# Latent stage of a hybrid layer on Trainium2: key latents first, query latents scaled after their product, sample queries on column groups

## The chip, the cores and the metric

The kernel runs on one core of one Trainium2 chip (trn2). The metric is device time in microseconds of one execution, lower is better. The core has five engines that matter here, each with its own instruction queue: TensorE (PE; its weight loads are listed as PEld), VectorE (DVE), ScalarE (ACT), GpSimd (POOL) and SyncE (SP), which issues the transfers between memory and the on-chip SBUF. TensorE writes into PSUM banks of 512 float32 columns.

## The reference

The program is a step of a small trunk of two layers over 288 tokens, 256 of a prompt and 32 of samples (8 sequences of 4). Each layer mixes three branches (a state-space branch "ssd", a recurrent branch "rwkv" and latent attention "mla") and ends in a feed-forward part. All branches read the same normalised rows through slices of one matrix `w_in`. What the change touches is the way from these rows to queries, keys and values:

```python
def rmsnorm(x, g, eps=NORM_EPS):
    y = xf * lax.rsqrt(jnp.mean(xf * xf, axis=-1, keepdims=True) + eps)
    return y * g

def mla_queries(cq, pos, q_a_g, w_q_b, q_norm_g):
    q = jnp.einsum('btr,rhe->bthe', rmsnorm(cq, q_a_g), w_q_b)
    q = jnp.concatenate([q[..., :MLA_NOPE], rope(q[..., MLA_NOPE:], pos)], axis=-1)
    return rmsnorm(q, q_norm_g)
...
    h = rmsnorm(x, p['norm_mix_g'])
    u = h @ p['w_in']
    q = mla_queries(u_mla[..., :MLA_Q_RANK], pos, p['mla_q_a_g'], p['mla_w_q_b'], p['mla_q_norm_g'])
    ckv = rmsnorm(u_mla[..., MLA_Q_RANK:MLA_Q_RANK + MLA_KV_RANK], p['mla_kv_a_g'])
    kpe = rope(u_mla[..., MLA_Q_RANK + MLA_KV_RANK:], pos)
```

The model width is 1024, the query rank 512, the key rank 256, the rotary part 64; there are 8 heads of 128 + 64. The ssd branch takes from `w_in` also 16 columns `dt`, one for each of its heads. The rwkv branch's output y (1024 features a token, 16 heads of 64) is normalised head by head, scaled, a bonus is added and the sum multiplied by a gate.

## The kernel before

`layer_program` runs the stages of a layer one after the other, in a loop over two layers; between two stages all engines meet. The stages that matter are, in order: `rwkv_tiles` (the recurrent scan), `mla_project` (called the latent stage here), `mla_qkv`, the attention stages, and later `ssd_project` and `ssd_tiles`.

Activations are kept transposed, features on the 128 partitions and 288 tokens along the row, and so are the latents. A float32 product of `w_in` columns with the rows is made of three passes over rounded halves (`product`, L301: weight head by row head, weight head by row rest, weight rest by row head). Each megabyte of weights (8 tiles of 128 rows, 256 columns) is fetched by SP, rounded by ScalarE into heads (a CAST), and split by VectorE into rests (a subtraction). A **unit** is 128 output features: 8 tiles x 3 passes = 24 matmuls of 288 columns.

The latent stage makes seven units in this order: four of query latents, two of key latents, and one for the rotary key (its 64 columns are loaded twice to fill 128). ScalarE copies each result from PSUM and squares it (L473, L474); TensorE sums the squares over features with a matrix of ones (L428, 6 instructions, each shown as 2 records since a plain float32 matmul takes two passes); ScalarE makes the inverse roots with Ln and Exp (L479, L481), each of which needs its own table loaded (ACT_TABLE_LOAD); VectorE applies gain and root to all six (L550). The key latents and the rotary key are turned token-major (L439, L434), the rotary key is rotated on VectorE (L541 to L546) and turned back (L444). SP writes both to memory, two stores for each (L383 to L387), and it also gathers ten cache pages in this stage (`gather_pages`). Between the units the recurrent branch's y is finished: mean and centring on VectorE (L520 to L522), squares on ScalarE (L462), inverse roots (L465, L467), scaling (L531), 32 transposes of 64x64 for each of two token tiles (`turn_y`, L399), then gain (L508), bonus (L513) and gate (L514). The first quarter of the first weights is fetched in `rwkv_tiles` (L2925) into `mla_w_first`.

`mla_qkv` makes keys, values and queries of three token tiles (two of 128 prompt tokens, one of the 32 samples; the samples need only queries). For a query tile, 12 matmuls (24 records) of 512 columns read `cqT`, the scaled query latents, as stationary operand. In the order of TensorE: keys and values of tiles 0 and 1, queries of tiles 0, 1 and 2, and then 64 transposes (`turns`, L621) whose results ScalarE copies out (L674, L676). Between a query pass and these turns, ScalarE keeps the queries (L654), VectorE rotates them (L695 to L700), ScalarE squares (L658), VectorE sums (L712), ScalarE makes inverse roots (L662, L664), and VectorE scales queries and keys (L714, L715). Each engine takes its instructions strictly in the order of the code.

`ssd_project` makes 10 double units and, as the eleventh load of 1 MB, one unit whose first 16 output features are dt (`dtT`, L1549).

## Time and profile before

| | us |
|---|---|
| median of 3 runs | 2954.49 |
| lowest, highest | 2952.33, 2960.16 |
| span of the profiled execution | 2949.8 |
| time of the kernel outside the span (median less span) | 4.7 |
| latent stage, layer 1 and layer 2 | 50.6, 51.73 |
| mla_qkv, layer 2 | 61.7 |

| engine | busy us | share of the span |
|---|---|---|
| TensorE | 2693.6 | 91% |
| VectorE | 1872.8 | 63% |
| ScalarE | 1352.8 | 46% |
| GpSimd | 841.2 | 29% |

A line of the timeline gives the start in the span, the time that a group of like instructions took, engine and source line, operation, what it writes and reads, the shapes, the count, and in brackets the idle time of the engine before it with the work or transfer that ended it. "x12" of a float32 matmul means six instructions. A releaser "PEq L232" is the meeting of the engines between two stages.

### The profile page before, as it was taken

Reading aid. Unit: us, or ns where it says so; the run is one execution under the profiler, and the core shown is the slowest. Engines: PE = TensorE matmul, PEld = TensorE weight load, DVE = VectorE, ACT = ScalarE, POOL = GpSimd, SP = SyncE. Lnnn points to the kernel's source line nnn. Section 1 sums busy time; section 2 is a strip of 40 time slices with the busy share of each in tenths; the row PEclk is TensorE's granted clock in tenths of the full one; section 3 lists DMA queues with packets and bytes.
Section 4 is the critical chain, followed back from the end, with each engine's and each line's share of the span. In section 5 each row is a group of like instructions: output and inputs, shape, how many; then the busy total and the mean of one; then the engine's idle time right before and its main releaser. Section 6 shows DMA issues by size and latency. Waiting matters only on the chain. (4 is left out here: it accounts for less than half of the span.)

```text
span 2949.8 us, 62087 instructions
## 1 busy us (share of the span) xinstructions
PE 2693.6 (91%) x24092; PEld 2462.7 (83%) x24092; DVE 1872.8 (63%) x3117; ACT 1352.8 (46%) x2294; POOL 841.2 (29%) x696
## 2 busy tenths in 40 slices
PE   7987889999999899899989878799999998998998
PEld 6876459999989689899978764599999895998998
DVE  4854457777766655489448454577777676554893
ACT  4733354545444244354357333555554442533542
POOL 0030009999910400000000300199999004000000
PEclk9999989999998999999989999899999998999999
DMA  5423459677545376365453243696866344764544
GB/s 134 110 59 105 138 100 148 117 129 122 83 79 161 97 202 168 104 166 139 126 115 101 65 132 112 115 141 115 139 106 104 74 141 124 199 172 108 161 133 120
DMA packets 838374, 365.86 MB, mean 124 GB/s; under 512 B 406189, under 2 KB 825558, under 8 KB 837512
## 3 DMA queue, kind: packets, MB, share of 16 engines
q1 hardware_dynamic: 835858, 360.77, 53.7%
q8 instruction: 184, 3.01, 0.4%
q10 hardware_dynamic: 2232, 1.26, 0.2%
q14 instruction: 100, 0.82, 0.1%
HBM read 342.63 MB, written 61.23 MB: 137 GB/s over the span
## 5 line engine op out<-in xcount | busy, mean ns | idle before, releaser
L1213 PE MATMUL key_banks<-w_kb_head,latent_T_head 128*128 128x352 f32 x1536 | 519.5, 338 | 9.7 <-DVE latent_T_rest L1341 9.7
L1213 PE MATMUL key_banks<-w_kb_head,latent_T_rest 128*128 128x352 f32 x1536 | 497.1, 324 | 0.0
L1213 PE MATMUL key_banks<-w_kb_rest,latent_T_head 128*128 128x352 f32 x1536 | 496.6, 323 | 0.0
L297 DVE TENSOR_TENSOR w_rests<-w_ring,w_heads 128x2048 fp32r<-128x2048 f32 (+1 forms) x150 | 321.6, 2147 | 146.9 <-ACT w_heads L291 146.7
L1355 DVE TENSOR_REDUCE w_kb<-key_sq 128x8 f32<-128x1024 f32 x256 | 311.2, 1216 | 12.4 <-ACT key_sq L1278 7.7
L1213 PEld LDWEIGHTS key_banks<-w_kb_head,latent_T_head 128*128 128x128 f32 x1536 | 290.5, 189 | 23.5 <-DVE latent_T_rest L1341 11.6
L1213 PEld LDWEIGHTS key_banks<-w_kb_rest,latent_T_head 128*128 128x128 f32 x1536 | 290.9, 189 | 0.0
L1213 PEld LDWEIGHTS key_banks<-w_kb_head,latent_T_rest 128*128 128x128 f32 x1536 | 289.8, 189 | 0.0
L291 ACT CAST w_heads<-w_ring 128x2048 fp32r<-128x2048 f32 (+1 forms) x150 | 268.4, 1792 | 42.8 <-ACT conv_last_rows L1934 19.7
L1033 POOL TENSOR_TENSOR rwkv_state_tmp<-rwkv_state,vec 128x1024 f32<-128x1024 f32 x64 | 153.3, 2395 | 455.6 <-POOLq L232 450.7
L1265 ACT CAST latent_T_head<-turn_bank 128x256 fp32r<-128x256 f32 x256 | 95.3, 372 | 400.6 <-PE key_banks L1217 392.2
L1278 ACT ACTIVATE key_sq<-key_banks 128x1056 f32<-128x1056 f32 x256 | 271.4, 1060 | 7.8 <-PE key_banks L1217 7.8
L2861 POOL TENSOR_TENSOR L_level<-L,const 128x1024 f32<-128x1024 f32 x12 | 28.1, 2366 | 793.5 <-DVE L L2867 793.5
L1341 DVE TENSOR_TENSOR latent_T_rest<-turn_bank,latent_T_head 128x256 fp32r<-128x256 f32 x256 | 108.2, 423 | 211.2 <-ACT latent_T_head L1265 211.0
L304 PE MATMUL ffn_banks<-h_heads_T,w_heads 128*128 128x288 f32 x704 | 212.8, 302 | 18.2 <-DVE h_rests_T L1950 13.8
L305 PE MATMUL ffn_banks<-h_rests_T,w_heads 128*128 128x288 f32 x704 | 209.6, 298 | 0.0
L306 PE MATMUL ffn_banks<-h_heads_T,w_rests 128*128 128x288 f32 x704 | 208.8, 297 | 0.0
L1036 POOL TENSOR_TENSOR rwkv_state_tmp<-rwkv_state_tmp 128x512 f32<-128x512 f32 (+4 forms) x320 | 197.9, 618 | 25.1
L304 PE MATMUL merge_banks<-out_heads,w_heads 128*128 128x288 f32 x512 | 150.9, 295 | 10.2 <-DVE out_rests L1751 5.2
L304 PEld LDWEIGHTS ffn_banks<-h_heads_T,w_heads 128*128 128x128 f32 x704 | 133.4, 189 | 22.8 <-DVE w_rests L297 18.0
L306 PE MATMUL merge_banks<-out_heads,w_rests 128*128 128x288 f32 x512 | 151.1, 295 | 0.0
L305 PE MATMUL merge_banks<-out_rests,w_heads 128*128 128x288 f32 x512 | 151.1, 295 | 0.0
(597 smaller groups left out, 7006.1 us busy)
## 6 DMA issues: line engine op xcount, KB each, us to landing
w_ring<-in_ffn_w_up_dram SPq DMA_DIRECT2D x88, 512.0 KB, 5.0
page_latents<-in_cache_kv_latent_dram SPq DMA_DIRECT2D x256, 128.0 KB, 2.4
latent_blocks<-page_latents SPq DMA_DIRECT2D x256, 128.0 KB, 3.9
latents<-page_latents SPq DMA_DIRECT2D x64, 512.0 KB, 8.4
w_ring<-in_w_in_dram SPq DMA_DIRECT2D x52, 512.0 KB, 3.8
w_ring<-in_w_gate_dram SPq DMA_DIRECT2D x46, 512.0 KB, 4.0
w_ring<-in_w_in_dram SPq DMA_DIRECT2D x20, 1024.0 KB, 5.9
w_ring<-in_ffn_w_down_dram SPq DMA_DIRECT2D x32, 384.0 KB, 3.3
```

The source lines that it names most:

```text
L291: nc.scalar.copy(heads[:, slot, 0:tiles * P], ring[:, slot, 0:tiles * P]).then_inc(rounded, 1)
L297: ops.tensor_tensor(rests[:, slot, 0:tiles * P], ring[:, slot, 0:tiles * P], heads[:, slot, 0:tiles * P].bitcast(F32), ALU.subtract).then_ ...
L304: nc.tensor.matmul(out, wh, xh, start=start, stop=False)
L305: nc.tensor.matmul(out, wh, xl, start=False, stop=False)
L306: return nc.tensor.matmul(out, wl, xh, start=False, stop=stop)
L1033: c(nc.gpsimd.tensor_tensor(tmp, S, over_v(n, t), ALU.mult))
L1036: c(nc.gpsimd.tensor_tensor(tmp[:, :, 0:w], tmp[:, :, 0:w], tmp[:, :, w:2 * w], ALU.add))
L1213: last = nc.tensor.matmul(kbank[:, 3 * x + n, 0:KB], c[:, x, r * P:(r + 1) * P], w[:, r, cols], start=r == 0 and m == 0, stop=r == 1 and m ...
L1265: nc.scalar.copy(ch[:, x, :], xbank[:, :]).then_inc(headed, 1)
L1278: nc.scalar.activation(sq[:, x, :], kbank[:, 3 * x:3 * x + 3, 0:KB], ACT.Square).then_inc(squared, 1)
L1341: nc.vector.tensor_tensor(cl[:, x, :], xbank[:, :], ch[:, x, :].bitcast(F32), ALU.subtract).then_inc(t_kept, 1)
L1355: nc.vector.tensor_reduce(ss[:, slot, j, :], sq[:, x, f:f + KW].rearrange("p (h e) -> p h e", e=NOPE), AX.X, ALU.add).then_inc(summed, 1)
```

## The change

Five things are done together.

1. The latent stage makes the key latents first. All 1 MB of their weights is fetched in `rwkv_tiles`, into the buffer that held the inverse Y of the scan. The order of TensorE is now: two key units, one unit that holds the rotary key (64 columns) and the dt columns of the ssd branch, the keys' square sums, two query units, the turns of rotary key and latents, the turn of y (tile 0), a query unit, the turn of y (tile 1), the rotary key back, the last query unit.
2. Only the key latents get their inverse root there. ScalarE keeps the query latents with their gain alone (`keep_query`) and writes their squares into `cq_sq`, which lies under the attention output. In `mla_qkv` TensorE sums these squares into one column a token (`latent_sums`, 12 instructions with 2 output columns), ScalarE makes the inverse roots (`latent_inverses`), and the queries are multiplied by them when they leave PSUM.
3. In `mla_qkv` the keys and values of tile 1 are made behind the queries of tiles 0 and 1, and the queries of the samples go as 12 matmuls with 32 weight columns each into three groups of 32 partitions of one bank (`sample_queries`).
4. `ssd_project` has ten loads and no dt unit.
5. On GpSimd are now the centring of y (two passes of 128x1024) and bonus and gate of tile 0 (two passes); the rotary keys of both prompt tiles are rotated in one set of six operations, 12 in place of 18.

```diff
@@ mla_project @@
+        kpe_w = ring[:, 1, 0:DT // 2, :].rearrange("p t (u n) -> p (t u) n", u=2)
...
+                for half, at in enumerate((OFF_MLA + QRANK + KVRANK, OFF_DT)):
+                    sp.dma_start(kpe_w[:, :, half * ROPE:(half + 1) * ROPE], w[:, at:at + ROPE].rearrange("(t p) n -> p t n", p=P)).then_inc(kpe_in, 16)
+                query_weights(0)
+                sp.wait_ge(split, 1)
+                query_weights(1)
...
+                pe.wait_ge(split, 1)
+                unit(KPE_BANK, kpe_heads, kpe_rests, 0).then_inc(kpe_made, 1)
+                pe.wait_ge(kv_kept, 2)
+                for t in range(2):
+                    last = nc.tensor.matmul(banks[:, SUM_BANK, 0:T], k.col("ones"), kv_sq[:, t, :], start=t == 0, stop=t == 1)
+                last.then_inc(summed, 1)
+                pe.wait_ge(split, 2)
+                for g in range(2):
+                    unit(g, heads[:, 1, :, :], rests[:, 1, :, :], g).then_inc(q_made, 1)
+                pe.wait_ge(kpe_kept, 1)
+                pe.wait_ge(inverse, 1)
...
+                def keep_query(i):
+                    act.wait_ge(q_made, i + 1)
+                    nc.scalar.activation(k.cqT[:, i, :], banks[:, i % 2, 0:T], ACT.Copy, scale=k.par("mla_q_a_g", i))
+                    nc.scalar.activation(k.cq_sq[:, i, :], banks[:, i % 2, 0:T], ACT.Square).then_inc(q_kept, 1)
...
+                act.wait_ge(q_in[1], 16)
+                nc.scalar.copy(heads[:, 0, :, :], ring[:, 1, :, :]).then_inc(rounded, 1)
+                act.wait_ge(kpe_made, 1)
...
+            @block.gpsimd
+            def _(pool):
+                for n in range(2):
+                    pool.wait_ge(y_mean, n + 1)
+                    nc.gpsimd.tensor_tensor(y[:, n, :].rearrange("p (h v) -> p h v", v=64), k.y_rows[:, n, :].rearrange("p (h v) -> p h v", v=64),
+                                            bc(mean[:, n, :], 64), ALU.subtract).then_inc(centred, 1)
+                cols = slice(0, P)
+                pool.wait_ge(y_scaled, 1)
+                nc.gpsimd.tensor_tensor(k.o_rwkv[:, :, cols], k.o_rwkv[:, :, cols], k.bonusT[:, :, cols], ALU.add).then_inc(y_added, 1)
+                pool.wait_ge(y_added, 1)
+                nc.gpsimd.tensor_tensor(k.o_rwkv[:, :, cols], k.o_rwkv[:, :, cols], k.gT[:, :, cols], ALU.mult)
@@ mla_qkv @@
+                def latent_sums():
+                    for n, (first, rows) in enumerate(TOK):
+                        for t in range(4):
+                            last = nc.tensor.matmul(banks[0:rows, SUM_BANK, 2 * n:2 * n + 2], k.cq_sq[:, t, first:first + rows], k.col("ones", 0, 2),
+                                                    start=t == 0, stop=t == 3, skip_group_check=True)
+                    last.then_inc(lat_summed, 1)
...
+                def sample_queries():
+                    for t in range(4):
+                        for j in range(3):
+                            last = nc.tensor.matmul(banks[32 * j:32 * j + 32, SAM_BANK, :], k.cqT[:, t, SEQ:T], w_q[:, t, j * 512:(j + 1) * 512],
+                                                    start=t == 0, stop=t == 3, skip_group_check=True)
+                    last.then_inc(sam_made, 1)
...
+                latent_sums()
                 keys_values(0)
...
                 queries(1)
                 pe.wait_ge(q_kept, 1)
-                queries(2)
                 pe.wait_ge(gain_kept, 1)
+                keys_values(1)
+                sample_queries()
+                pe.wait_ge(k_kept, 2)
...
+                latent_inverses()
                 keep_keys_values(0)
+                keep_queries(0)
+                square_queries(0)
+                inverses(0)
+                keep_queries(1)
+                square_queries(1)
                 keep_keys_values(1)
-                norm_queries(0)
+                inverses(1)
@@ ssd_project @@
-    ORDER = [NZ, NZ + 1, 0, NZ + 2, NZ + 3, 1, NZ + 4, NZ + 5, 2, 3, NU]
+    ORDER = [NZ, NZ + 1, 0, NZ + 2, NZ + 3, 1, NZ + 4, NZ + 5, 2, 3]
...
-                act.wait_ge(dt_made, 1)
-                nc.scalar.copy(k.dtT[:, :], banks[0:SSD_HEADS, 6, 0:T])
@@ rwkv_tiles @@
-                sp.dma_start(k.first_w[:, :, :], k.ldram("w_in")[0:2 * P, OFF_MLA:OFF_MLA + 256].rearrange("(t p) n -> p t n", p=P)).then_inc(k.first_in, 16)
+                sp.wait_ge(made["ta"], 2)
+                sp.wait_ge(made["tk"], 2)
+                sp.dma_start(k.first_w[:, :, :], k.ldram("w_in")[:, OFF_MLA + QRANK:OFF_MLA + QRANK + KVRANK].rearrange("(t p) n -> p t n", p=P)).then_inc(k.first_in, 16)
```

TensorE at the end of the latent stage and in `mla_qkv`, before: `mla_sq` are the squares, `ckvT` the key latents, `kpe_tm` the rotary keys by token, `ssd_yT` here holds the value weights, `w_q_b` the query weights.

```order
L428 MATMUL mla_banks<-mla_sq,const 128x288 x6
L434 MATMUL mla_banks<-const,mla_w 128x64 x2
L434 MATMUL mla_banks<-const,mla_w 32x64
L439 MATMUL mla_banks<-const,ckvT 128x128 x4
L439 MATMUL mla_banks<-const,ckvT 32x128 x2
L444 MATMUL mla_banks<-const,kpe_tm 64x128 x2
L444 MATMUL mla_banks<-const,kpe_tm 64x32
```

The same engine after the change, from the turns of the rotary key on; the units around them are left out of the first piece.

```order
L426 MATMUL mla_banks<-const,kpe_T 128x64 x2
L426 MATMUL mla_banks<-const,kpe_T 32x64
L431 MATMUL mla_banks<-const,ckvT 128x128 x4
L431 MATMUL mla_banks<-const,ckvT 32x128 x2
L396 MATMUL mla_banks<-const,qnT 64x64 x32
L304 MATMUL mla_banks<-h_heads_T,mla_w_heads 128x288
```

The square sums of all six latents stood behind every product and ahead of the transposes; now the transposes stand between the second and third query unit, and products follow them.

ScalarE in the second half of the latent stage, before (`mla_w_heads` are rounded weights, `cqT` the query latents, `mla_w_first_rest` the inverse roots):

```order
L454 CAST mla_w_heads<-mla_w 128x8x128
L473 COPY ckvT<-mla_banks 128x288
L474 ACTIVATE mla_sq<-mla_banks 128x288
L473 COPY ckvT<-mla_banks 128x288
L474 ACTIVATE mla_sq<-mla_banks 128x288
L476 COPY mla_w<-mla_banks 64x288
L479 ACT_TABLE_LOAD
L479 ACTIVATE mla_w_first_rest<-mla_banks,const 128x288 x2
L481 ACT_TABLE_LOAD
L481 ACTIVATE mla_w_first_rest<-mla_w_first_rest 128x576
```

And after, from the cast of the second query weights (L469) to the keeping of the first query latent (L450):

```order
L469 CAST mla_w_heads<-mla_w 128x2048
L471 COPY kpe_T<-mla_banks 64x288
L472 COPY dtT<-mla_banks 16x288
L474 ACT_TABLE_LOAD
L474 ACTIVATE kv_inverse_root<-mla_banks,const 128x288
L476 ACT_TABLE_LOAD
L476 ACTIVATE kv_inverse_root<-kv_inverse_root 128x288
L478 ACT_TABLE_LOAD
L478 ACTIVATE ssd_yT<-ssd_yT,const 128x32
L480 ACT_TABLE_LOAD
L480 ACTIVATE ssd_yT<-ssd_yT 128x32
L450 ACTIVATE cqT<-mla_banks,params 128x288
```

The roots moved from behind the last unit to the middle, behind the last cast of weights, and stand ahead of the query latents in ScalarE's queue.

TensorE in `mla_qkv`, before:

```order
L597 MATMUL qkv_banks<-w_kb,ckvT 128x512 x4
L597 MATMUL qkv_banks<-ssd_yT,ckvT 128x512 x4
L626 MATMUL qkv_banks<-const,qk_gain 128x32
L627 MATMUL qkv_banks<-const,qk_gain 64x32
L597 MATMUL qkv_banks<-w_kb,ckvT 128x512 x4
L597 MATMUL qkv_banks<-ssd_yT,ckvT 128x512 x4
L605 MATMUL qkv_banks<-w_q_b,cqT 128x512 x24
L605 MATMUL qkv_banks<-w_q_b,cqT 32x512 x12
```

and after:

```order
L607 MATMUL qkv_banks<-const,o_mla 128x2 x8
L607 MATMUL qkv_banks<-const,o_mla 32x2 x4
L616 MATMUL qkv_banks<-w_kb,ckvT 128x512 x4
L616 MATMUL qkv_banks<-ssd_yT,ckvT 128x512 x4
L654 MATMUL qkv_banks<-const,o_mla 128x32
L655 MATMUL qkv_banks<-const,o_mla 64x32
L624 MATMUL qkv_banks<-w_q_b,cqT 128x512 x24
L616 MATMUL qkv_banks<-w_kb,ckvT 128x512 x4
L616 MATMUL qkv_banks<-ssd_yT,ckvT 128x512 x4
L631 MATMUL qkv_banks<-w_q_b,cqT 32x512 x12
```

Keys and values of tile 1 moved behind the queries, and the tiny sums (L607) stand first.

## Rows read from the trace of the kernel before

**Rows 1.** The page's first line

```profile
span 2949.8 us, 62087 instructions
```

**Rows 2.** Stage borders: one stretch by engine (layer 1), first instructions (layer 2)

```profile
275.40:326.00 50.60, 36.08 (x320) 33.29 (x320) 32.93 (x61) 22.26 (x35) 0.00 (x0) 0.82 0.50 153
...
1741.06 0.62 ACT L457 CAST mla_w_heads<-mla_w_first 128x512 fp32r<-128x512 f32 x1 [1.51 <-PEq L232]
...
1792.79 1.19 PE L597 MATMUL qkv_banks<-w_kb,ckvT 128*128 128x512 f32 x1 [3.58 <-PEq L232]
```

**Rows 3.** Timeline of PE in the latent stage, layer 2

```profile
1773.38 2.08 PE L399 MATMUL mla_banks<-const,qnT 64*64 64x64 f32 x64
1778.69 3.08 PE L428 MATMUL mla_banks<-mla_sq,const 128*128 128x288 f32 x12
...
1787.05 1.54 PE L439 MATMUL mla_banks<-const,ckvT 128*128 128x128 f32 x6 [4.97 <-DVE ckvT L550]
```

**Rows 4.** Stretch: busy PE, PEld, DVE, ACT, POOL, PEclk, DMA share, GB/s

```profile
1744.40:1755.10 10.70, 9.27 (x36) 8.83 (x37) 6.69 (x8) 6.84 (x7) 0.00 (x0) 0.50 0.67 219
```

**Rows 5.** Timeline of SP's DMA queue around the latent stage, layer 2

```profile
1736.02 0.45 SPq L2925 DMA_DIRECT2D mla_w_first<-in_w_in_dram  x1
...
1760.93 0.58 SPq L326 DMA_DIRECT2D page_latents<-in_cache_kv_latent_dram  x1
...
1781.16 0.50 SPq L326 DMA_DIRECT2D page_latents<-in_cache_kv_latent_dram  x1
...
1791.39 0.33 SPq L387 DMA_DIRECT2D out_dram<-kpe_tm  x1
```

**Rows 6.** DMA issues from 1736 to 1760: count, KB each, median us to landing

```profile
mla_w<-in_w_in_dram SPq DMA_DIRECT2D x2, 1024.0 KB, 8.7
w_kb<-in_mla_w_kb_dram SPq DMA_DIRECT2D x1, 1024.0 KB, 5.9
```

**Rows 7.** Timeline of ACT in the latent stage, layer 2

```profile
1750.90 1.90 ACT L454 CAST mla_w_heads<-mla_w 128x2048 fp32r<-128x2048 f32 x1 [1.28 <-DMA mla_w<-in_w_in_dram]
1752.82 1.28 ACT L465 ACT_TABLE_LOAD   x1
```

**Rows 8.** Timeline of DVE in the latent stage, layer 2

```profile
1766.92 2.64 DVE L508 TENSOR_SCALAR o_rwkv<-mla_banks,params 128x128 f32<-128x128 f32 x8 [2.19 <-PE mla_banks L399]
1769.59 1.23 DVE L513 TENSOR_TENSOR o_rwkv<-o_rwkv,bonusT 128x1024 f32<-128x1024 f32 x1
```

**Rows 9.** GpSimd's passes on the page, and POOL beside DVE in ssd_tiles, layer 2

```profile
L1033 POOL TENSOR_TENSOR rwkv_state_tmp<-rwkv_state,vec 128x1024 f32<-128x1024 f32 x64 | 153.3, 2395 | 455.6 <-POOLq L232 450.7
...
2433.52 4.03 POOL L3200 TENSOR_TENSOR ssd_yT<-xbcT,skip_by_feature 128x2304 f32<-128x2304 f32 x1 [0.30 <-DVE skip_by_feature L3260]
...
2436.28 1.33 DVE L3265 SCALAR_TENSOR_TENSOR dt<-dt,softplus 128x48 f32<-128x48 f32 x1 [2.52 <-ACT softplus L3170]
2437.64 0.22 DVE L3267 SCALAR_TENSOR_TENSOR dt_a<-dt,a 128x48 f32<-128x48 f32 x1
```

**Rows 10.** Timelines of mla_qkv, layer 2, and of two other stages' small matmuls

```profile
1808.72 31.18 PE L605 MATMUL qkv_banks<-w_q_b,cqT 128*128 128x512 f32 x72
...
1819.22 1.44 ACT L654 COPY q_tm<-qkv_banks 128x1536 f32<-128x1536 f32 x1 [7.91 <-PE qkv_banks L605]
...
1841.68 0.67 ACT L674 ACTIVATE qnT<-qkv_banks,qk_gain_T 128x512 f32<-128x512 f32 x1
...
890.63 7.00 PE L1468 MATMUL ssd_banks<-qa,ssd_yT 128*128 128x32 f32 x32 [1.54 <-PEq L232]
...
530.49 1.07 PE L1242 MATMUL misc_bank<-latents,w_kb 128*32 128x257 f32 x16
```

**Rows 11.** ssd_project's end, layer 2: next PE row, SP's wait, the stretch behind

```profile
2432.73 0.76 PE L2985 MATMUL ssd_banks<-const,dtT 16*128 16x16 f32 x12 [2.03 <-PEq L232]
...
SPq L1441 <- DMA out_dram<-conv_last_rows: 1.8, 1, 1.8
...
2434.00:2438.00 4.00, 4.00 (x33) 3.35 (x36) 1.65 (x3) 2.66 (x6) 4.00 (x6) 0.57 0.97 263
```

346 lines of the change are left out of this document (169 added, 177 removed).

## The prediction

> **What bounds the kernel now.** I read the page first: the span is 2949.8 us [rows 1], and TensorE is busy through nine tenths of it, so time can be won where TensorE waits. Then the timeline at the borders of the two stages that the change rewrites: the latent stage begins with ScalarE's first cast and ends with TensorE's first matmul of the qkv stage. It takes 1792.79 - 1741.06 = 51.73 us in layer 2 and 50.6 in layer 1 [rows 2]. All times t below count from 1741.06.
>
> Read TensorE's rows of that stage [rows 3]. The first product starts at t = 3.4 [rows 4]. The seven units of 24 matmuls and the two turns of y (64 records, 2.08 us each) are over at t = 37.6, where the square sums begin (1778.69). From there to the qkv stage, 14.1 us pass in which TensorE does 3.08 + 0.4 + 1.54 + 0.8 us of small matmuls and idles for the rest: square sums, two roots with their table loads (1.28 us each), the rotation of the keys, six scalings (the idle of 4.97 us before the row at 1787.05), transposes, two copies, and four stores that SP issues one behind the other, the last at 1791.39, t = 50.3 [rows 5]. **This tail of 14.1 us is what the stage is bound by.** The other 37.6 us are TensorE work with weights arriving just ahead of it; its clock is at 0.50, that is 1.2 GHz, in the first 10.7 us of work [rows 4].
>
> **The change part by part.**
>
> Head of the stage. 1 MB of weights is fetched in the stage before instead of 256 KB. The old transfer was issued at 1736.02, t = -5.0 [rows 5]; 1 MB lands in 5.9 to 8.7 us in this stretch [rows 6], so at t = 0.9 to 3.7. I take 0.9, since no other big transfer runs beside it at that time; the other end goes to the range. Four casts of at most 0.62 us [rows 2] and four splits about as long follow at once, the first product starts at t = 2.2, and the idle of 1.4 us between pieces is gone. The 48 matmuls of the key units at 0.24 us each (the spacing at 1.2 GHz: 10.7 us of work for 36 of them, with one gap [rows 4]), the last ones faster, end at t = 13.0. The unit of rotary keys and dt: 24 at 0.133 (full clock) = 3.2, t = 16.2. The square sums are now 4 records instead of 12, 3.08/12 x 4 = 1.0, t = 17.2. Two query units follow, 6.4 us: t = 23.6. Their weights are issued at t = 1 to 2 behind the small rotary-key transfers, land by t = 12, are cast by 14 and split by 15.2 to 16, so they are ready.
>
> The queue that decides is **ScalarE's**. It takes its instructions in order, and the cast of the second query weights stands ahead of the keeping of the rotary keys and of both roots. SP issues those weights only when the split of the rotary-key weights is done, because they take the same buffer. That split waits for the engine pair below; I put it at t = 9.0. Landing at 6.5 us (between 5.9 and 8.7, nearer to the lower end as the two 1 MB transfers no longer start together) gives 15.6; cast 1.9: 17.4; two copies: 18.1; key root and its two table loads 2 x 1.28 + 0.9: 21.6 [rows 7]; root of y, two loads more: 24.7; first scaling of y 1.2: 25.9. TensorE has done the transposes of rotary keys and latents (0.4 + 1.5) at 25.5, so the two meet. Then turn 2.08: 28.0; unit 3.2: 31.2; turn: 33.3; three transposes back 0.8: 34.1; last unit 3.2: **t = 37.2**. The total of products is as before, and the stretch holds 3.7 us of small matmuls that stood in the tail.
>
> Tail. Behind the last product there are two ScalarE copies (0.8 us, t = 38.0), and on VectorE, behind the second turn at 33.3, eight scalings 2.64 and two passes of 1.23 [rows 8]: t = 38.4. The passes of the other half are GpSimd's now, 28.0 + 2.64 + 2 x 2.4 = 35.5 [rows 9], and hidden. The four stores no longer close the stage: latents' rows are kept at about t = 30, keys rotated at about 28. SP reaches them behind ten pages of the gather. Before, the first was issued at 1760.93 and the tenth at 1781.16, 2.25 us a page [rows 5]; now they start at about t = 11.5 and end at 34. The stores go out by 36. With the 0.9 us between the last work and the next stage's first instruction the stage is 39.5 us, **12.2 less** (head -0.4, tail -11.8). Layer 1 starts with the same idle and runs the same chain, its slack at the head a little larger: 38.8, **11.8 less**.
>
> What moves to GpSimd meets VectorE. In the dt stage a GpSimd pass over two tiles in SBUF runs from 2433.52 for 4.03 us; a tiny VectorE operation with two SBUF inputs that starts beside it takes 1.33 us and ends 0.06 us after it, while its like takes 0.22 with GpSimd at a single-input copy [rows 9]. So a VectorE operation with two inputs waits out the GpSimd one. In the new stage the centring of y (2.4 us each on GpSimd, from t = 5.4 and 10.5) stands against the split of the rotary-key weights and the split of the first query weights. That is +1.2 us on the former, already in the 9.0 above, and through the second weights it reaches the end of the stage: without it I get 37.8 for the stage instead of 39.5. The Trainium skill says of this pair ("SBUF — State Buffer", SBUF: two separate sides) that the port is an exclusive lock held for a whole instruction and the loser fully blocks; it speaks against this move, and the trace agrees with the 1.33 us.
>
> The qkv stage, 61.7 us before. TensorE's matmuls there are not its end: what sets it is the chain from the first kept query tile (1819.22) to the first turned one (1841.68), 22.5 us of ScalarE and VectorE in turn, then some 12 us of turning out [rows 10]. Now the first query pass comes earlier: before it started 15.9 us into the stage and took 24 x 0.433 = 10.4, done at 26.4. Now key and value of tile 1 (7.2 us) stand behind it, but 24 tiny matmuls for the query latents' square sums stand ahead; the nearest row is 32 records with 128-wide weights and 32 columns in 7.00 us, 0.22 each [rows 10], so 2.2 to 4.4 us. First tile made at 21.3 to 23.5, a lead of 3 to 5 us. But the square and sum of keys(1) (1.49 + 1.75 and a hand-over) now lie in the chain behind queries(1): 22.5 + 3.8 = 26.3. Start of turning out: 47.6 to 49.8 against 48.9. TensorE then idles 5 us before the turns; where it idled 2.5 us in layer 2, the next turns ran at half clock, costing about a microsecond. Fewer query matmuls (the sample pass shrinks from 10.4 to 3.5 us) lie under this chain and bring nothing. I take **0 for the stage, ±2**. The column groups: four groups of 32 columns run in 0.0625 us a record of 257 columns [rows 10], where one alone would take 0.433 x 257/512 = 0.217, so groups overlap; three should give about 3.5 us. If they did not, sample queries end at 22.4 + 10.4 + 7.2 + 10.4 = 50.4, 1.7 us late.
>
> ssd_project loses a unit of 24 matmuls (3.2 us), its load, cast and split. TensorE ended there at 2430.7 and started the next stage at 2432.73 [rows 11]; but SP waits there for the stores of the conv rows, 1.8 us, to about 2431.85 [rows 11]. Their issue hangs on ScalarE's copies ahead of the dt unit, and they stay. So the unit was covered and its removal brings 0. TensorE now idles 5.4 us before the next stage, whose clock was at 0.57 from its second to its sixth microsecond even so [rows 11]; the cost is 0 to 1.7 us a layer, I take +0.5.
>
> Sum: -12.2 - 11.8 + 0 + 2 x 0.5 = -23.0. The profiled execution is 2949.8 + 4.7 outside the span = 2954.5, the median of the runs shown. 2954.5 - 23.0 = **2931.5 us**.
>
> **The rivals.**
> (a) The change gives more: no port conflict at the places that count (-1.7 a layer), a qkv stage 1 us shorter, no clock loss in the dt stage: 2931.5 - 3.4 - 2 - 1 = 2925. For it: the operations overlap only if their starts fall so.
> (b) The second query weights land late. At 8.7 us instead of 6.5, or with the first megabyte at t = 3.7 instead of 0.9, ScalarE's queue and with it both roots shift by 2 to 3 us a layer: 2936.5. For it: 8.7 is the median of this very pair [rows 6]. Against: they no longer share their start.
> (c) The column groups don't overlap: +1.7 a layer, 2935; [rows 10] speak against it.
> (d) **Slower than before**: the new order keeps TensorE at 1.2 GHz in the latent stage, since more small transposes and waits lie between its units. Then five units cost 2.6 us more each, and sums, turns and transposes (8 us) up to twice: 39.5 + 13 + 8 = 60.5, 9 us over before, 2973. It turns the sign once over 12 of these 21 us are lost. Against it: the old order has the same turns of narrow matmuls between its units, and the unit behind the second turn still ran at 0.133 us a matmul.
>
> **How the numbers follow.** Forecast (2928 to 2935) 0.52, (a) 0.22, (b) 0.17, (c) 0.05, (d) 0.04. The range takes in (a), (b) and (c) and the bounds of the terms (±2 for qkv a layer, late weights): 2922 to 2944. A measurement of this kernel can tell about 0.3%, 8.9 us, from no change, so faster means under 2945.6: all of the first four but the far ends of (b) with a lost qkv gain, 0.92; within 0.3% 0.05; slower 0.03.
>
> **What would show it.** Right: the latent stage at 39 to 40 us with TensorE's first product at t = 2 to 3; the last product within 3 us of the next stage; root of the keys by t = 22; ScalarE's wait for the second query weights under 2 us; GpSimd's centring ending at the same instant as a stretched split on VectorE; the 12 narrow sample matmuls x 2 records in under 4 us; chain from first kept query to turning out at 26; ssd_project's end unchanged. Wrong: stores still last in the stage; granted clock at 0.5 after t = 13; the qkv stage longer than 64 us.

## The result, and the profile after

| | before | changed |
|---|---|---|
| median, us | 2954.03 (4 runs, 2952.33 to 2960.16) | 2918.15 (4 runs, 2913.44 to 2922.59) |
| span of the profiled execution, us | 2949.8 | 2920.8 |
| latent stage, layer 1 and 2, us | 50.6, 51.7 | 38.8, 39.0 |

The ratio is 0.9879, 95% interval 0.9857 to 0.9901: the kernel is 35.9 us faster. The forecast was 2931.5, 23 us less than before, and its range ended at 2922. The sign and the mechanism in the rewritten stages held. The size did not.

The page of the changed kernel, its span and TensorE's line, and from the timeline of layer 2 ScalarE's first and last instruction of the latent stage and the first ones of ScalarE and TensorE in the next stage:

```profile
span 2920.8 us, 62019 instructions
...
PE 2677.7 (92%) x24076; PEld 2459.3 (84%) x24076; DVE 1857.5 (64%) x3091; ACT 1354.8 (46%) x2302; POOL 856.5 (29%) x704
...
1729.11 2.18 ACT L458 CAST mla_w_heads<-inverse_then_mla_w 128x512 fp32r<-128x512 f32 x4 [1.50 <-PEq L232]
...
1766.43 0.40 ACT L451 ACTIVATE o_mla<-mla_banks 128x288 f32<-128x288 f32 x1
...
1768.08 1.28 ACT L684 ACT_TABLE_LOAD   x1 [1.25 <-PEq L232]
1768.12 2.26 PE L607 MATMUL qkv_banks<-const,o_mla 128*128 128x2 f32 x24 [2.13 <-PEq L232]
```

The stage now takes 1768.08 - 1729.11 = 38.97 us, where [rows 2] give 51.73. Behind the last product TensorE's queue is empty for 2.13 us only; the tail of sums, roots and transposes of [rows 3] is gone from the end. TensorE's own small matmuls and the first product, with the SP and VectorE rows that answer to [rows 5, 8]:

```profile
1730.50 0.61 PE L304 MATMUL mla_banks<-h_heads_T,mla_w_heads 128*128 128x288 f32 x1 [4.12 <-DVE mla_w_rests L532]
...
1742.82 1.13 PE L418 MATMUL mla_banks<-kv_sq,const 128*128 128x288 f32 x4
...
1750.28 0.39 PE L426 MATMUL mla_banks<-const,kpe_T 64*128 64x64 f32 x3
1750.60 0.87 PE L431 MATMUL mla_banks<-const,ckvT 128*128 128x128 f32 x6
1753.12 3.40 PE L396 MATMUL mla_banks<-const,qnT 64*64 64x64 f32 x64 [1.64 <-DVE qnT L549]
...
1760.03 2.08 PE L396 MATMUL mla_banks<-const,qnT 64*64 64x64 f32 x64
...
1762.37 0.33 SPq L383 DMA_DIRECT2D out_dram<-kpe_tm  x1
...
1766.10 1.22 DVE L528 TENSOR_TENSOR o_rwkv<-o_rwkv,gT 128x1024 f32<-128x1024 f32 x1
```

The last store is issued at 1762.37, 5.7 us ahead of the next stage; VectorE's last pass and ScalarE's last copy close the stage. TensorE waits 1.64 us for the scaled y, and the turn behind that wait is slow (3.40 us, the second one 2.08). A wait there does not always do this: in layer 1 of `again` (an execution of the same kernel, below) TensorE waited 2.53 us and the turn took 2.08.

I set the stage boundaries of every profile side by side (in layer 1, layer 2). Three executions of the kernel before and four of the changed one:

| stage | before, us | changed, us | difference of the means, both layers |
|---|---|---|---|
| latent | 50.6, 51.7; 52.1, 51.5; 51.7, 50.5 | 38.8, 39.0; 38.0, 38.1; 37.7, 37.2; 40.8, 39.1 | -25.6 |
| qkv | 61.9, 61.6; 61.8, 61.7; 61.1, 61.4 | 62.3, 60.4; 60.2, 62.4; 61.7, 60.1; 60.5, 61.5 | -0.9 |
| ssd_project and ssd_tiles | 153.4 on average | 153.5 on average | +0.3 |
| all other stages | | | -8 |
| span | 2949.8, 2951.0, 2951.4 | 2920.8, 2912.2, 2917.0, 2916.8 | -34.0 |

So 26 us are where the prediction looked for them, and 8 lie elsewhere. Of the other stages the change touches only `rwkv_tiles`, where the larger prefetch is issued; it has -0.8 of the 8.

### The profile page after: what moved, and what is told of

It reads as the page before. It is cut to its first block and busy times, and to the rows that moved or that the text cites. A ratio compares the mean times of both kernels' runs of the same rounds, so it can differ in the third digit from the quotient of the medians.

```text
span 2920.8 us, 62019 instructions
## 1 busy us (share of the span) xinstructions
PE 2677.7 (92%) x24076; PEld 2459.3 (84%) x24076; DVE 1857.5 (64%) x3091; ACT 1354.8 (46%) x2302; POOL 856.5 (29%) x704
## 5 line engine op out<-in xcount | busy, mean ns | idle before, releaser
L1269 PE MATMUL key_banks<-w_kb_head,latent_T_head 128*128 128x352 f32 x1536 | 519.3, 338 | 10.6 <-DVE latent_T_rest L1397 10.6
L1089 POOL TENSOR_TENSOR rwkv_state_tmp<-rwkv_state,vec 128x1024 f32<-128x1024 f32 x64 | 153.4, 2396 | 236.4 <-POOLq L232 231.6
```

The lines of the kernel that those rows point to most:

```text
L1089: c(nc.gpsimd.tensor_tensor(tmp, S, over_v(n, t), ALU.mult))
L1269: last = nc.tensor.matmul(kbank[:, 3 * x + n, 0:KB], c[:, x, r * P:(r + 1) * P], w[:, r, cols], start=r == 0 and m == 0, stop=r == 1 and m ...
```

## The experiments

Each kernel is the changed one with one edit, unless it says otherwise. Ratios are against the kernel before, timed on the same chip in the same session.

**The two kernels again.** `again` is the changed kernel as it is; `before_again` the kernel before.

> The changed kernel as it is, for a second profile and more times. Theory A (untouched stages differ by chance, through the granted clock at their beginnings): latent stages again 38.5 to 39.5 us each, and the untouched stages sum within 4 us of either first profile but not in the same places; ratio to the kernel before about 0.991 (26 to 29 us gained), less than the 36 us of the first comparison. Theory B (the change also speeds stages it does not touch): ratio again 0.988 (35 us), and the same untouched stages are shorter as in the first profile (prompt attention in layer 1 by 3, value absorption in layer 2 by 1.6).

> The kernel before as it is, for a second profile. Both theories: latent stages 50.6 and 51.7 us. Theory A: its untouched stages scatter by up to 3 us each against its own first profile, with the granted clock of the stretch saying which; time within 0.3% of the other runs of the kernel before. Theory B: prompt attention in layer 1 again at 38.2 us.

Measured: `again` 2917.7 us, ratio 0.988 (0.9855 to 0.9905); `before_again` 2954.63, 1.0 (0.9984 to 1.0016). The size of the gain repeats here. Later sessions on other chips gave 0.9911 (`again_2`, 27.1 us, what theory A had said) and 0.9897 (`again_3`, 34.7 us), so the ratio does not tell A from B. Theory A's mechanism is seen in the profiles: with one code, layer 1's prompt attention took 35.2 us in one execution and 32.6 in the other. The stretches (length, then busy time of PE, PEld, DVE, ACT, POOL, then the granted clock, the DMA share and GB/s), first the changed kernel, then `again`:

```profile
379.00:414.20 35.20, 32.41 (x153) 21.89 (x153) 21.82 (x75) 19.74 (x55) 0.00 (x0) 0.81 0.56 120
```

```profile
369.20:401.80 32.60, 27.80 (x152) 19.80 (x153) 21.60 (x75) 19.72 (x55) 0.00 (x0) 0.95 0.60 130
```

VectorE and ScalarE do the same work in both; TensorE is busy 4.6 us longer at 0.81 than at 0.95. Over all profiles this stage of layer 1 has five lengths, whatever the kernel, and each goes with its clock: 32.6 at 0.95, 35.2 at 0.81, 36.7 at 0.77, 38.2 at 0.73, 39.8 at 0.70.

**GpSimd and VectorE.** `y_on_dve` takes all of y off GpSimd:

```diff
-            @block.gpsimd
-            def _(pool):
...
+                    nc.vector.tensor_tensor(by_head(y, n), by_head(k.y_rows, n), bc(mean[:, n, :], 64), ALU.subtract).then_inc(centred, 1)
...
-                    if n == 1:
-                        dve.wait_ge(y_scaled, 2)
-                        c(nc.vector.tensor_tensor(k.o_rwkv[:, :, cols], k.o_rwkv[:, :, cols], k.bonusT[:, :, cols], ALU.add))
+                    dve.wait_ge(y_scaled, n + 1)
+                    c(nc.vector.tensor_tensor(k.o_rwkv[:, :, cols], k.o_rwkv[:, :, cols], k.bonusT[:, :, cols], ALU.add))
```

> The changed kernel with centring, bonus and gate of y all on VectorE again, nothing on GpSimd in the latent stage. Theory port (the exclusive pair costs): no 2.9 us split of the first query weights, it is back at 2.3; but VectorE carries 2 x 1.2 more before the third split. Latent stage 38 to 39 us, the kernel 0 to 2 us faster. Theory load (VectorE's own time is the limit): the latent stage 1 to 2.5 us longer each, since the centring passes stand ahead of the split of the rotary-key and query weights on VectorE.

Measured: 2914.49 us, ratio 0.9876 (0.9851 to 0.99), beside 2917.7 of the unedited kernel: no difference that this measurement can tell. The latent stages took 37.2 and 39.0 us. Moving four passes to GpSimd brought nothing that shows. That what it saves on VectorE is lost at the port is a reading that fits the rows below; no run separates the two. The changed kernel's two engines in layer 2, and then the same place in layer 1 of a later profile (`again_3`):

```profile
1738.25 1.90 POOL L497 TENSOR_TENSOR qnT<-o_rwkv,ssd_yT 128x1024 f32<-128x1024 f32 x1 [2.67 <-DVE ssd_yT L514]
...
1739.40 2.91 DVE L538 TENSOR_TENSOR mla_w_rests<-mla_w,mla_w_heads 128x2048 fp32r<-128x2048 f32 x1 [1.23 <-ACT mla_w_heads L462]
```

```profile
278.78 2.29 DVE L538 TENSOR_TENSOR mla_w_rests<-mla_w,mla_w_heads 128x2048 fp32r<-128x2048 f32 x1
...
278.86 3.98 POOL L497 TENSOR_TENSOR qnT<-o_rwkv,ssd_yT 128x1024 f32<-128x1024 f32 x1 [2.50 <-DVE ssd_yT L514]
...
282.86 1.06 ACT L455 ACTIVATE y_squares_then_qrT<-qnT 128x1024 f32<-128x1024 f32 x1 [1.84 <-POOL qnT L497]
```

In the first pair GpSimd began first: it takes its 1.90 us, and the split takes 2.91 instead of 2.29. In the second VectorE began 0.08 us earlier: the split takes 2.29, GpSimd 3.98 instead of 1.90, and ScalarE, whose next instruction needs y, idles 1.84 us with the whole queue behind it. That stage is the longest of the eight, 40.8 us. This is what the Trainium skill says in "SBUF — State Buffer", SBUF: two separate sides: whichever starts first gets the pair for the whole instruction and the other fully blocks; both orders agree with it here.

**Column groups.** `one_group_at_a_time` swaps the loops of the sample queries:

```diff
-                    for t in range(4):
-                        for j in range(3):
+                    for j in range(3):
+                        for t in range(4):
```

> The changed kernel with the sample queries' loops swapped, so that four matmuls in a row write the same group of 32 partitions. Theory overlap: the 12 matmuls (24 records) take 10 us instead of 3.5 to 4, as one group alone is no faster than a full tile; the turns start up to 2 us later a layer, the kernel 0 to 4 us slower. Theory no overlap (each matmul costs the same in whichever order): no difference in their duration nor in the time.

Measured: 2916.45 us, 0.9882 (0.9857 to 0.9907). TensorE's row for the 12 matmuls, in the changed kernel (layer 2) and in this one (layer 1; layer 2 took 7.11 us too):

```profile
1807.38 3.63 PE L631 MATMUL qkv_banks<-w_q_b,cqT 128*32 128x512 f32 x24
```

```profile
348.72 7.11 PE L631 MATMUL qkv_banks<-w_q_b,cqT 128*32 128x512 f32 x24
```

The groups overlap when consecutive matmuls go to different ones: 0.151 us a record, 3.63 in all, as forecast from [rows 10]. One group after the other took 7.11 us, not the 10 expected, 0.296 a record on average. The starts in the trace say why. The records of one group stand 0.43 us apart, as those of a full tile do. But the last four records of a group run beside the first four of the next one, so 24 records take the time of 16. Two stretches of 1.7 us, counted for these matmuls alone, the first inside one group and the second at a border:

```profile
348.70:350.40 1.70, 1.68 (x4) 0.47 (x5) 1.00 0.30 96
350.60:352.30 1.70, 1.70 (x11) 0.48 (x9) 1.00 0.34 83
```

The kernel before had all 24 records of the sample pass in one group: 0.43 us apart, 10.49 us. The 3.5 us do not reach the end: the matmuls lie under the chain on ScalarE and VectorE.

**The root of the query latents.** `query_root_in_stage` puts it back into the latent stage:

```diff
                 unit(1, heads[:, 0, :, :], rests[:, 0, :, :], 1).then_inc(q_made, 1)
+                pe.wait_ge(q_kept, 4)
+                for t in range(4):
+                    last = nc.tensor.matmul(banks[:, SUM_BANK, 0:T], k.col("ones"), k.cq_sq[:, t, :], start=t == 0, stop=t == 3)
+                last.then_inc(q_summed, 1)
...
+                nc.scalar.activation(inv[:, :], banks[:, SUM_BANK, 0:T], ACT.Ln, bias=k.col("eps"), scale=1.0 / QRANK).then_inc(inverse, 1)
...
+                for r in range(4):
+                    nc.vector.tensor_tensor(k.cqT[:, r, :], k.cqT[:, r, :], inv[:, :], ALU.mult)
...
-                latent_sums()
                 keys_values(0)
```

> The changed kernel with the query latents' root back in the latent stage: behind the last unit the four squares are summed (8 records of 0.26), Ln and Exp with two table loads (2 x 1.28 + 1.0), and four multiplications on VectorE (0.45 each); the qkv stage has no latent sums and no latent roots. Theory tail (the late root is where the gain comes from): the latent stage 6 to 8 us longer, 44 to 46 us; the qkv stage 2 to 4 us shorter since the first query tile is made that much earlier; the kernel 6 to 10 us slower than the changed one. Theory order (the order of units and the prefetch bring the gain, the root is a detail): less than 3 us slower in all.

Measured: 2927.26 us, 0.9906 (0.9877 to 0.9934). Its timeline behind the last unit of layer 2:

```profile
1759.76 2.21 PE L448 MATMUL mla_banks<-o_mla,const 128*128 128x288 f32 x8 [0.89 <-ACT o_mla L456]
...
1762.00 0.50 ACT L499 ACTIVATE kv_inverse_root<-mla_banks,const 128x288 f32<-128x288 f32 x1 [1.00 <-PE mla_banks L448]
1762.52 1.28 ACT L501 ACT_TABLE_LOAD   x1
1763.81 0.44 ACT L501 ACTIVATE kv_inverse_root<-kv_inverse_root 128x288 f32<-128x288 f32 x1
...
1764.29 1.56 DVE L576 TENSOR_TENSOR cqT<-cqT,kv_inverse_root 128x288 f32<-128x288 f32 x4 [4.08 <-ACT kv_inverse_root L501]
```

This is the tail again, from 1759.7 to 1765.9. The latent stages are 42.9 and 44.8 us, 5.2 above the mean of the changed kernel, and the qkv stages 58.8 and 59.2, 2.1 below theirs. By the profiles the late root is thus worth about 3 us a layer of the 13. The total does not show it: the changed kernel ran at 2927.35 us and 0.9911 on this chip (`again_2`, in a later session), so the 6 to 10 us expected did not appear, and the theories are told apart by stage lengths alone. The prefetch is worth some 2.8 (below). If the parts add, 7 are left for the order of units with key latents first, which lets their root, transposes, rotation and stores run under the query units. That part was not undone alone, so its share is a remainder and not measured.

**Keys and values of tile 1 ahead of its queries.** `kv1_first`:

```diff
-                queries(1)
                 pe.wait_ge(q_kept, 1)
                 pe.wait_ge(gain_kept, 1)
                 keys_values(1)
+                queries(1)
...
+                keep_keys_values(1)
                 keep_queries(1)
                 square_queries(1)
-                keep_keys_values(1)
...
-                queries(1)
                 keys(1)
+                queries(1)
```

> The changed kernel with keys and values of tile 1 made ahead of queries of tile 1 in qkv, and their square and sum ahead of the queries' on ScalarE and VectorE. Theory chain (the chain from the first kept query tile to the first turn sets the stage, and keys(1) behind queries(1) costs 3.8 us of it): the turns start 2 to 3.5 us earlier, each qkv stage 57 to 59 us instead of 60 to 62. Rival: queries(1) are then made 7 us later (TensorE) and the chain waits for them: no gain or up to 2 us worse.

Measured: 2935.07 us, 0.9935 (0.9914 to 0.9955). My own step fell and the rival stood, stronger than priced: qkv stages of 64.8 and 67.9 us, where the changed kernel has 60.1 to 62.4. ScalarE in layer 2:

```profile
1784.93 1.54 ACT L693 ACTIVATE q_tm<-qkv_banks,o_mla 128x1536 f32<-128x1536 f32 x1 [8.31 <-PE qkv_banks L624]
...
1804.17 1.54 ACT L693 ACTIVATE q_tm<-qkv_banks,o_mla 128x1536 f32<-128x1536 f32 x1 [3.49 <-PE qkv_banks L624]
...
1814.51 0.67 ACT L718 ACTIVATE qnT<-qkv_banks,qk_gain_T 128x512 f32<-128x512 f32 x1
```

ScalarE waits 3.49 us for the second query tile, and everything that must follow it (rotation, square, sum, two roots) then starts late: 29.6 us from the first kept tile to the first turned one. The changed kernel needs 24.9:

```profile
1790.33 1.54 ACT L693 ACTIVATE q_tm<-qkv_banks,o_mla 128x1536 f32<-128x1536 f32 x1 [8.75 <-PE qkv_banks L624]
...
1815.20 0.67 ACT L718 ACTIVATE qnT<-qkv_banks,qk_gain_T 128x512 f32<-128x512 f32 x1
```

**The dt unit.** `ssd_unit_back` restores `ssd_project` as it was (dt is made twice, the second one is used):

```diff
-    ORDER = [NZ, NZ + 1, 0, NZ + 2, NZ + 3, 1, NZ + 4, NZ + 5, 2, 3]
+    ORDER = [NZ, NZ + 1, 0, NZ + 2, NZ + 3, 1, NZ + 4, NZ + 5, 2, 3, NU]
...
+                act.wait_ge(dt_made, 1)
+                nc.scalar.copy(k.dtT[:, :], banks[0:SSD_HEADS, 6, 0:T])
```

> The changed kernel with the dt unit of ssd_project put back (dt is made twice, the second one is used). Theory cover: ssd_project stays at 80.4 us since the stores of the conv rows end it, and the first microseconds of ssd_tiles run at a higher granted clock: the kernel within 2 us of the changed one. Rival (the unit cost something): 1 to 3 us slower a layer.

Measured: 2929.8 us, 0.9902 (0.9875 to 0.9928), on another chip than the first kernels, and one stretch of its profile stood out (ssd_tiles of layer 2 at 79.7 us, clock 0.80, where all others have 72.6 to 75.8). So both were run side by side:

> The changed kernel once more, on the chip of this comparison, since the last four kernels (2927 to 2935 us) ran beside the kernel before only and on another chip than the first ones. Theory chip (a chip grants its clock a little differently, so the four are all some us high): 2920 to 2930 us here if this chip is like the second one, latent stages again at 37 to 39 us. Theory edits (the four edits cost 10 us each): 2914 to 2921 us.

> The dt unit of ssd_project put back, once more, beside the changed kernel on one chip. Theory cover (the stores end ssd_project, so the unit is free): within 3 us of the changed kernel, ssd_project at 80 us in both. Theory clock (the unit's extra TensorE work costs elsewhere, through the granted clock): ssd_project the same, and again a ssd_tiles or merge stage that is 3 to 6 us longer at a granted clock of 0.80 to 0.97, the kernel 6 to 12 us slower.

Measured: `again_2` 2927.35 us (0.9911, 0.9881 to 0.9941), `ssd_unit_back_2` 2922.41 (0.9886, 0.9852 to 0.992), ssd_project 80.3 and 80.4 us in layer 1, 80.2 and 79.9 in layer 2. The long ssd_tiles did not come back (73.8). The unit was free, as forecast. `again_2` came out as theory chip had said (2920 to 2930): in the session on this chip the unedited kernel stood at 2927 us, against 2918 in those on others, so the four kernels timed on it (2927 to 2935) are not each 10 us worse by their edits. Whether it is the chip itself is not shown; the kernel before stood at 2954 to 2956 on it, as elsewhere. SP's waits at the end of the changed kernel's stage show the same end as [rows 11]:

```profile
SPq L1497 <- DMA out_dram<-conv_last_rows: 1.8, 1, 1.8
```

**The prefetch.** `quarter_ahead` fetches 256 KB ahead and three quarters in the stage; `weights_earlier` (on top of `y_on_dve`) issues the megabyte four cache pages sooner:

```diff
+                for q in range(1, 4):
+                    sp.dma_start(k.first_w[:, 2 * q:2 * q + 2, :], w[2 * q * P:2 * (q + 1) * P, OFF_MLA + QRANK:OFF_MLA + QRANK + KVRANK].rearrange("(t p) n -> p t n", p=P)).then_inc(piece_in[q], 16)
```

```diff
-                copied = gather_pages(sp, k, GATHER["tiles"], gathered)
+                gather_pages(sp, k, GATHER["tiles"][:-4], gathered)
                 sp.wait_ge(made["ta"], 2)
                 sp.wait_ge(made["tk"], 2)
...
+                gather_pages(sp, k, GATHER["tiles"][-4:], gathered)
```

> The changed kernel with only a quarter of the key weights fetched ahead (256 KB, as before the change) and three quarters at the start of the latent stage. Theory head is small: products start at the same time, one gap of 1 to 2 us between pieces; the later megabytes land 2 us later and shift ScalarE's queue; latent stage 1 to 4 us longer each (39 to 42). In executions where the scan before it is quick, the late landing of the megabyte (ScalarE's wait of 2 to 6.5 us at the stage's start in the profiles so far) goes away, a gain of 0.5 to 4 us there. Kernel 0 to 5 us slower.

> The changed kernel with y on VectorE and the prefetch of the key weights issued four cache pages (8.5 us) earlier in the scan's stage. Theory: the prefetch is issued behind the gather and not behind the inverse, so it comes late when the scan ends early (waits of 0.6, 1.0 and 5 us seen at the start of the latent stage); here it is always landed and ScalarE's wait at the start is the 1.5 us of the meeting. Latent stage 37 to 38 us each, the kernel 0 to 4 us faster than the changed one. Rival: the scan's stage gets longer, as SP waits for the inverse and its gather ends later.

Measured: `quarter_ahead` 2929.05 us (0.9906, 0.9887 to 0.9926), latent stages 42.1 and 40.6 against 38.6 on average, so the full prefetch is worth some 2.8 us a layer by the profiles; in the total, beside the 2927.35 of `again_2`, no difference can be told. `weights_earlier` 2922.12 us (0.989, 0.9858 to 0.9922) beside 2927.35: again no difference that can be told, but the mechanism shows. The first cast of layer 1 in `one_group_at_a_time`, in `again_3` and in `weights_earlier`:

```profile
274.02 2.18 ACT L458 CAST mla_w_heads<-inverse_then_mla_w 128x512 fp32r<-128x512 f32 x4 [6.53 <-DMA inverse_then_mla_w<-in_w_in_dram]
```

```profile
269.89 2.18 ACT L458 CAST mla_w_heads<-inverse_then_mla_w 128x512 fp32r<-128x512 f32 x4 [2.69 <-DMA inverse_then_mla_w<-in_w_in_dram]
```

```profile
255.04 1.06 SPq L2963 DMA_DIRECT2D inverse_then_mla_w<-in_w_in_dram  x1
...
274.36 2.18 ACT L458 CAST mla_w_heads<-inverse_then_mla_w 128x512 fp32r<-128x512 f32 x4 [1.53 <-PEq L232]
```

SP reaches the prefetch only behind 44 cache pages. When the scan ends early, that can be too late, here by 5.0 and by 1.2 us over the 1.5 us of the meeting. In `weights_earlier` it is issued 19.3 us ahead of the stage (4.4 in `again_3`) and is in time, and the latent stages are 37.4 and 37.1. Its scan stage took 109.9 us, not the 106.3 of the two late cases; by my estimate it would have been in time with 3.6 us less too, since 1 MB landed in 5.9 to 8.7 us in [rows 6].

**The 8 us elsewhere.** `before_third` is another execution of the kernel before. `changed_padded` and `before_padded` put idle ScalarE passes ahead of the first cast of the latent stage, `again_3` is their control:

```diff
+                pad = Chain(act, padded)
+                for n in range(12):
+                    pad(nc.scalar.activation(y_sq[:, 0, :], k.y_rows[:, 0, :], ACT.Square))
                 act.wait_ge(k.first_in, 16)
```

> The kernel before once more, for a third profile of its untouched stages. Theory chance: feed-forward with the next layer's entry (394 us in both profiles so far, 388 to 393 in the changed one) and layer 1's prompt attention (38.2 in both) scatter here as they do in the changed kernel, 388 to 395 and 32.7 to 39.8. Theory systematic: again 394 and 38.2.

> The changed kernel with 12 idle passes of ScalarE (squares of y, overwritten later) ahead of the first cast in each latent stage, so that the stage is as long as before the change: 51 to 53 us instead of 38. Theory position (the clock of later stages depends on where in time they begin): the untouched stages go back to what they were, feed-forward with entry to 394.4 in this profile, and the kernel loses more than the 27 us of padding: 2950 to 2956. Theory change (what the new stages leave behind lets the later ones run faster): that stage stays at 392.6 or below and the kernel is 2943 to 2948.

> The kernel before with 6 idle passes of ScalarE ahead of the first cast in each latent stage, some 6 us more. Latent stage 56 to 58. Theory position: feed-forward with entry leaves 394.4 for another of its levels (392.6 or 388.6) or some other level, and the kernel's loss differs from the 12 us of padding by 2 to 6 either way. Theory change: 394.4 as in all profiles of the kernel before, and 12 us slower, 2966.

> The changed kernel, control on the same chip: 2914 to 2927 us; latent stages 37 to 39; feed-forward with entry 392.6 for the fourth time if its level is fixed by what stands before it, 388.6 in some executions if it is by chance.

Measured: `before_third` 2954.05 us; `changed_padded` 2944.13 (0.9969, 0.9947 to 0.9991); `before_padded` 2960.81 (1.0038, 1.0021 to 1.0055); `again_3` 2918.5 (0.9897, 0.9869 to 0.9926). Below are the feed-forward stage of layer 1 (with the entry of the next layer) and the 10 us stretch that begins 170 us into it, for the kernel before, the changed one, `changed_padded` and `again_3`:

```profile
1238.30:1632.60 394.30, 355.50 (x2480) 338.66 (x2480) 275.39 (x547) 206.96 (x364) 0.00 (x0) 0.94 0.50 130
1408.30:1418.30 10.00, 7.12 (x35) 6.88 (x33) 5.50 (x5) 4.45 (x5) 0.00 (x0) 0.66 0.63 167
```

```profile
1226.40:1618.70 392.30, 353.68 (x2480) 336.78 (x2481) 275.44 (x547) 207.00 (x364) 0.00 (x0) 0.96 0.50 131
1396.40:1406.40 10.00, 7.66 (x48) 7.60 (x49) 5.25 (x4) 4.22 (x5) 0.00 (x0) 0.83 0.72 190
```

```profile
1233.10:1621.50 388.40, 350.35 (x2480) 334.11 (x2480) 275.38 (x547) 206.96 (x364) 0.00 (x0) 0.96 0.50 132
1403.10:1413.10 10.00, 9.47 (x73) 9.33 (x73) 5.43 (x5) 3.79 (x4) 0.00 (x0) 1.00 0.81 223
```

```profile
1221.50:1610.20 388.70, 350.52 (x2480) 334.12 (x2481) 275.31 (x547) 206.97 (x364) 0.00 (x0) 0.97 0.51 132
1391.50:1401.50 10.00, 9.42 (x72) 9.30 (x73) 5.44 (x5) 3.84 (x5) 0.00 (x0) 1.00 0.86 224
```

TensorE has the same 2480 matmuls in each of these stages, and VectorE and ScalarE are busy for the same time within 0.2 us. In the stretch the clock is 0.66, 0.83 or 1.00. In the stretch, or just ahead of it, TensorE waits once for VectorE's split of the weights, for the same time in each profile. The first matmul behind it, in the kernel before, the changed one and `again_3`:

```profile
1411.45 0.58 PE L304 MATMUL ffn_banks<-ffn_act_heads,w_heads 128*128 128x288 f32 x1 [2.88 <-DVE w_rests L297]
```

```profile
1398.74 0.58 PE L304 MATMUL ffn_banks<-ffn_act_heads,w_heads 128*128 128x288 f32 x1 [2.89 <-DVE w_rests L297]
```

```profile
1392.08 0.38 PE L304 MATMUL ffn_banks<-ffn_act_heads,w_heads 128*128 128x288 f32 x1 [2.88 <-DVE w_rests L297]
```

Behind it, 24 matmuls of the kernel before start 0.24 us apart (the low clock, 1.2 GHz) and 13 of the changed kernel, while in `again_3` they are 0.13 apart from the second on. So the same wait was followed by about 5.8, 3.1 or 0 us of low clock.

The feed-forward stage took 394.3 to 394.5 us in three profiles of the kernel before, but 389.3 in `before_padded`. It took 392.3 to 392.7 in three profiles of the changed kernel, 388.7 in the fourth, and 388.4 in `changed_padded`. The other eight kernels of this section lie between 388.3 and 392.8. `before_third` went both ways: prompt attention of layer 1 left 38.2 for 36.7 us, as theory chance had said, and feed-forward stayed at 394.4, as theory systematic had. Padding the changed kernel came out as theory change had said (2944 us and 388.4), padding the kernel before as theory position had said (another level than 394.4). Neither theory holds for both, so the level is not tied to the kernel alone, nor to the length of what stands before alone.

The padding was also shorter than planned. In `changed_padded` the two latent stages are 49.5 us each, 19.1 us more in sum than in `again_3` and 21.9 more than the mean of the changed kernel; the time rose by 25.6. It still stands 9 us under the kernel before, while its latent stages are only 3.7 us shorter in sum. In `before_padded` they are 54.0 and 55.2 us, 6.4 us more than the mean in sum, and the time rose by 7.7.

How firm are the 8 us? All stages but latent, qkv, ssd_project and ssd_tiles sum to 2416 to 2421 us in three profiles of the kernel before and to 2406 to 2414 in four of the changed one, but to 2402 to 2423 in the eight unpadded kernels with one edit, so profiles alone do not separate them. Over all executions on record the medians are 2954.5 (kernel before) and 2918.8 (changed, 17), 35.7 us apart; by session the distance was 27, 35, 36 and 39 us. What is shown is that unchanged work took other times at another granted clock behind the same waits. **What sets the clock's level there stays open.**

## Why the prediction was right and where it was wrong

- **The bound.** Right. The tail was the limit; it went from 14.1 to 2.1 us (last product done at t = 36.9, next stage at 38.97), forecast 2.3.
- **The chain inside the new stage.** Each point came somewhat sooner than forecast, in layer 2 of the first profile: first product t = 1.4 (2.2), key units done 10.7 (13.0; full clock came at t = 7.3 already), second query weights cast from 13.4 (15.6), y scaled for the first turn at 24.0 (25.9), last product 36.9 (37.2), next stage 38.97 (39.5; by its own terms, 38.4 + 0.9, the forecast should have been 39.3). Part of the lead was spent on one thing that I had not in the sum: TensorE and the scaled y did not meet, TensorE waited 1.64 us, and the turn behind it was 1.3 us longer. In all eight stages of the four profiles it waited, 1.4 to 2.6 us, and in four of them the turn was slow (2.6 to 3.4 us). Over the four profiles the stages average 38.6 against my 39.15: 1 us in all.
- **The port.** Right in kind, and the place changes from stage to stage. In layer 2 of the first profile it is 0.6 us on the weights' split and nothing on the rotary-key split. Over the eight stages of the four profiles the rotary-key split took 1.23 to 2.57 us (0.8 to 1.3 longer than 1.23 in five), the weights' split 2.9 to 3.6 instead of 2.29 in seven, and in the eighth GpSimd paid 2 us. GpSimd's centring took 1.90 us, not the 2.4 that I took from [rows 9].
- **qkv at 0.** The sum held (-0.45 a layer). The latent sums cost 2.3 to 4.1 us (forecast 2.2 to 4.4), the chain 24.9 us (forecast 26.3), TensorE's idle before the turns was 3.9 us, and the 56 turns behind it took 10.3 to 11.3 us over the four profiles, 9.6 to 10.6 before, which gave part of the lead back. My row for that cost was misread: the idle ahead of the turns in layer 2 of the kernel before was 1.48 us, not 2.5. That keys(1) belongs ahead of queries(1) would have been the natural reading of my sum; `kv1_first` shows that it is wrong.
- **ssd_project at 0.** Right. The clock loss of +0.5 a layer in ssd_tiles did not show (73.2 against 73.3), 1 us.
- **The rivals.** (b) did not come: in layer 2 of the first profile ScalarE did not wait for the second query weights at all. Nor did (d): the clock is 0.87 to 0.93 over the new latent stages, where before it was 0.80 to 0.85. (a) was the right side but not far enough: its 2925 lies 7 us above the result. Its price for a stage without conflict, 37.8, is met by `weights_earlier`, which has the megabyte in time and no GpSimd passes: 37.1 and 37.4. (c) did not come: 3.63 us for the sample queries, forecast 3.5, though the row I took it from has 1.07 / 16 = 0.067 us a record and not 0.0625.
- **What failed: the stages that are not in the sum.** The step is the sum itself. "Sum: -12.2 - 11.8 + 0 + 2 x 0.5 = -23.0" has terms for the latent, qkv and ssd stages. The other stages, some 2420 us, enter at nothing, and no reason is given. They measured -8 us in the profiles, the feed-forward stage of layer 1 alone -2.9 (394.4 us at a clock of 0.94, then 391.6 at 0.95 to 0.97). The terms that are in the sum measured -26 against -23: latent -25.6 for -24.0, qkv -0.9 for 0, ssd +0.3 for +1. With these alone the kernel would have come to 2954 - 26 = 2928, inside the range. Why the other stages were faster stays open, as said above.
- **What failed: the range.** It held the bounds of the terms and nothing for the other stages. One kernel's executions scatter by 15 to 24 us (17 of the changed one lie between 2913.3 and 2928.3, those of the kernel before between 2941.5 and 2965.8), and a median of four moves with them. In the session of `again_2` the same kernel stood at 2927.35, inside the range. That the first session gave 2918 and not 2927 is nothing that the prediction could have told.
- **A slip that did no harm: 4.7 us "outside the span".** It took one execution's span from the median of others. In every execution on record whose span is known the part outside is 1.7 to 1.9 us (2922.59 - 2920.8; 2913.95 - 2912.2; 2952.86 - 2951.0), so the execution of [rows 1] was a quick one, about 2951.6. The base 2954.5 was right all the same, since it was the median itself: 2954.03 in the comparison.

## What to carry to other kernels

Look at what stands between a stage's last large product and the next stage's first: small sums, roots with their table loads, transposes and stores there cost their full time, and they can be brought under other products by making what needs them first, and by applying a per-row factor where the result leaves PSUM; the stage went from 51 to 39 us here. Before moving a link of a chain forward, ask which of the other engines must wait for what is pushed back: two engines that alternate are as late as the later input. And a range needs the scatter of all that the change leaves alone, not only the bounds of the terms in the sum.

## What the runs showed of the hardware

- One code at one place runs at a few recurring lengths: layer 1's prompt attention at 32.6, 35.2, 36.7, 38.2 or 39.8 us with a granted clock of 0.95, 0.81, 0.77, 0.73 or 0.70; a 10 us stretch of the feed-forward part at 0.66, 0.83 or 1.00.
- Twelve matmuls with 32-column weights, three column groups in turn, took 0.151 us a record. All in one group they took 0.43 a record, as long as full tiles (10.49 us, the kernel before). With four matmuls in a row to the same group it was 0.296 on average: 0.43 within a group, with four records of two neighbouring groups side by side at each border.
- The same wait of TensorE, 2.88 us for the same split in the feed-forward stage, was followed by 24, 13 or no matmuls at the low clock in different executions.
- 24 records with 128-column weights and 2 output columns took 2.26 to 4.07 us, 0.09 to 0.17 each, below the 0.22 of the row with 32 columns in [rows 10].
- A GpSimd pass of 128x1024 took 1.90 us with one operand of 16 values spread over it and 2.37 with two full ones.
